# Token shift moved into the projection's eviction, and a new order of work inside a recurrent round

## The reference, cut to what matters

```python
h = rms_norm(x, g_pre)
z = h @ w_in
zs, zg_r, q, k, v, qi, ki, wi, zg_a, m_r, m_a = _split(z, SPLITS)
...
prev = jnp.concatenate([shift0[:, None, :].astype(zs.dtype), zs[:, :-1]], axis=1)
xs = zs + (prev - zs) * mu_shift
r, k, v, zw, za = _split(xs, (R_WIDTH, R_WIDTH, R_WIDTH, DECAY_RANK, ICLR_RANK))
w_log = -jax.nn.softplus(-(w0 + jnp.tanh(zw) @ w2).astype(f32)) - 0.5
a = jax.nn.sigmoid((a0 + za @ a2).astype(f32))
kk = k * ph(k_k); kk = kk / jnp.maximum(jnp.sqrt(jnp.sum(kk * kk, ...)), 1e-12)
k = k * (1.0 + (a - 1.0) * ph(k_a))
y, s_final = rwkv7_scan(r, decay, k, v, kk, kk * a, s0)
... group norm of y, plus sum(r * k * r_k) * v, times silu(zg)
return y, s_final, zs[:, -1]        # the last unshifted row is an output too
```

## Time and profile before

| what | value |
|---|---|
| time, median of 3 runs (lowest, highest) | 3446.24 us (3445.89, 3452.47) |
| profiled execution, its own time | 3446.67 us |
| its span, first to last instruction | 3445.1 us |
| busy: PE, DVE, ACT, POOL | 3162.6, 2162.1, 1105.0, 521.5 us |
| 0 to 1454 us (fro): PE, DVE, ACT, POOL busy | 1428.4, 1127.6, 331.9, 105.9 us |
| 1454 to 2087 us (attention): the same | 551.7, 405.6, 273.9, 112.5 us |
| 2087 to 2621 us (rwk): the same | 400.0, 362.5, 350.4, 243.6 us |
| 2621 to 3446 us (merge): the same | 782.5, 266.4, 148.8, 59.5 us |

### The profile page before, as it was taken

How to read it: one execution, slowest core, us unless ns; L and a number is a source line. 1 busy time by engine, 2 the same in 40 slices (tenths; PEclk the granted TensorE clock), 3 DMA queues, 4 the chain that set the end, 5 groups by cost and what they waited for, 6 DMA issues and landing times. The chain is left out here.

```text
span 3445.1 us, 66198 instructions
## 1 busy us (share of the span) xinstructions
PE 3162.6 (92%) x25784; PEld 1917.1 (56%) x25784; DVE 2162.1 (63%) x4342; ACT 1105.0 (32%) x2313; POOL 521.5 (15%) x732
## 2 busy tenths in 40 slices
PE   8999999999999999869999865877876999999998
PEld 4544445555555555446666544777765555555553
DVE  2017889999999999658776554677772444432221
ACT  4135660000000000135555324677762211111221
POOL 3331000000000000021111132455542000000000
PEclk9999999999999999979999976889897999999999
DMA  5232111111111111132111181222215211221110
GB/s 161 72 93 66 43 41 57 56 55 58 55 57 62 55 58 55 59 96 67 43 44 33 49 271 47 57 62 66 64 31 158 100 52 54 64 78 58 49 40 25
DMA packets 215817, 233.54 MB, mean 68 GB/s; under 512 B 28665, under 2 KB 191028, under 8 KB 215012
## 3 DMA queue, kind: packets, MB, share of 16 engines
q1 hardware_dynamic: 147960, 110.07, 11.8%
q0 software_dynamic: 23696, 59.79, 6.0%
q10 hardware_dynamic: 43868, 59.62, 5.0%
HBM read 158.75 MB, written 70.63 MB: 67 GB/s over the span
## 5 line engine op out<-in xcount | busy, mean ns | idle before, releaser
L409 PE MATMUL fro_acc<-h_t,fro_w 128*128 128x416 f32 x3280 | 1174.6, 516 | 0.0
L409 PEld LDWEIGHTS fro_acc<-h_t,fro_w 128*128 128x128 f32 x3280 | 614.5, 190 | 543.1 <-issue 536.1
L692 DVE TENSOR_SCALAR_CACHE_REDUCE fro_work<-scores,fro_real 128x384 uint8<-128x384 f32 (+6 forms) x462 | 656.2, 1474 | 2.1
L516 ACT ACTIVATE fro_out<-fro_acc 128x416 f32<-128x416 f32 (+3 forms) x230 | 118.0, 513 | 794.1 <-PE fro_acc L409 711.6
L3105 DVE CUSTOM_DVE_ANT_0 att_seen<-att_ps,scores 128x512 f32<-128x512 f32 (+3 forms) x320 | 181.4, 608 | 99.8 <-PE att_ps L2991 99.5
L2169 PE MATMUL mrg_po<-mrg_wo,mrg_mrg 128*128 128x512 f32 (+1 forms) x544 | 238.8, 597 | 4.6 <-DVE mrg_mrg L2274 4.6
L2201 PE MATMUL mrg_pg<-mrg_wg,mrg_x_t 128*128 128x512 f32 (+1 forms) x544 | 236.3, 592 | 0.0
L658 DVE SCALAR_TENSOR_TENSOR scores<-fro_work,w_idx,scores 128x512 f32<-128x512 f32 (+3 forms) x280 | 188.0, 671 | 39.2 <-ACT fro_work L573 12.2
L3075 ACT ACTIVATE att_seen<-att_seen,att_shift 128x128 f32<-128x128 f32 (+15 forms) x128 | 152.6, 1194 | 83.2 <-DVE att_shift L3113 83.2
L2169 PEld LDWEIGHTS mrg_po<-mrg_wo,mrg_mrg 128*128 128x128 f32 (+1 forms) x544 | 101.5, 187 | 139.1 <-issue 134.1
L573 ACT ACTIVATE fro_work<-fro_wk 128x512 f32<-128x512 f32 (+3 forms) x320 | 144.5, 540 | 90.7 <-PE fro_wk L482 89.8
(11 more groups left out here) (449 smaller groups left out, 4523.5 us busy)
## 6 DMA issues: line engine op xcount, KB each, us to landing
z_t<-fro_out ACTq DMA_DIRECT2D x180, 208.0 KB
fro_w<-in_w_in SPq DMA_DIRECT2D x41, 512.0 KB, 4.1
mrg_m_in<-z_t POOLq DMA_DIRECT2D x56, 256.0 KB, 3.5
scores<-in_cache_kv POOLq DMA_DIRECT2D x108, 128.0 KB, 3.1
rwk_zi<-z_t SPq DMA_DIRECT2D x80, 129.0 KB, 2.6
z_t<-fro_out ACTq DMA_DIRECT2D x45, 192.0 KB
scores<-in_x_prompt SPq DMA_DIRECT2D x16, 512.0 KB, 8.4
mrg_x<-in_x_prompt SPq DMA_DIRECT2D x16, 512.0 KB, 3.5
```

Of the source, the lines that this page charges most:

```text
L409: last = pe.matmul(acc[e % 2][:, 0:CW], w[block_no % 3][:, kk, :], h_t[:, kk, CW * g:CW * g + CW], start=(kk == 0), stop=(kk == KD - 1))
L692: chain.mark(dve.tensor_scalar(junk[b % 2][:, 0:n], scores[:, c:c + n], realf[:, b:b + 1], None, op, ALU.add, accum_out=count[:, b:b + 1]))
```

## The change: what it does, and the diff

The token shift is taken out of the recurrent stage and done once, in fro, when the 65 accumulators of the shifted blocks are evicted. For such an accumulator ACT now makes three copies where it made one: the raw columns into `out[:, 1:]`, the columns scaled by 1 - mu into `shifted`, and one column (zero, or the last of the group before) into `out[:, 0]`; the last group of a block adds a one-column copy into `tail`. POOL multiplies `out` by mu and adds it to `shifted`, and ACT starts the DMA of shifted group i-1 at the end of the eviction of group i, waiting for POOL (`mixed`). `out` of a shifted group is free when POOL has mixed it, no longer when a DMA has landed. POOL gets its own copy of the list of steps, with `store_keys` and `load_qi` dealt between the shifts.

In the recurrent stage `zi`, `pm`, `own_part`, `shifted` and `add_parts` are gone; SP loads `xs` and `vx` ready-made into three buffers each. ACT's `take_square(1)` and `take_keys` now stand ahead of `exps`, `take_square(2)` ahead of `spread_norms` and `take_values`; PE's `norms` come behind `square(3)`; DVE's `power(3)` comes ahead of `unit_key` and `mixed_key`, and `power(4)` behind them but ahead of `scaled_keys`. The zero column of `z_t` is no longer written, and the output of the last raw row comes from `tail`.

```diff
@@ fro, GpSimd
-            for q in range(NT - 1):
-                store_keys(q)
+            def shift(i):
+                e, j, g = E_SHIFT + i, i // CG, i % CG
+                m = CW if g < CG - 1 else CP
+                mu = PR["mu_shift"][0] + j
+                pool.wait_ge(raw_ok, i + 1)
+                pool.wait_ge(first_ok, i + 1)
+                pool.tensor_tensor(out[e % 3][:, 0:m], out[e % 3][:, 0:m], k.param[:, mu:mu + 1].to_broadcast([P, m]), ALU.mult).then_inc(faded, 1)
+                pool.wait_ge(faded, i + 1)
+                pool.wait_ge(evicted, e + 1)
+                pool.tensor_tensor(shifted[i % 2][:, 0:m], shifted[i % 2][:, 0:m], out[e % 3][:, 0:m], ALU.add).then_inc(mixed, 1)
...
             load_qi(0)
             load_qi(1)
-            store_keys(NT - 1)
+            shift_steps(2)
+            for gr in range(2):
+                for b in range(4):
+                    shift_steps(2)
+                for half in range(2):
+                    shift_steps(5)
+                if gr == 0:
+                    store_keys(0)
+            shift_steps(5)
+            for n in range(NT):
+                shift_steps(2)
+                if n >= 1:
+                    store_keys(n)
             store_keys(NT)
-            for b in range(2, NT):
-                load_qi(b)
+            for u, (b, sl, width) in enumerate(index_units()):
+                if sl == 0 and 2 <= b + 1 < NT:
+                    load_qi(b + 1)
+                for four in range(2):
+                    shift_steps(pace[2 * u + four])
+            shift_steps(B_STEPS)
@@ fro, ScalarE
+            def store_shift(i):
+                e, j, g = E_SHIFT + i, i // CG, i % CG
+                m = CW if g < CG - 1 else CP
+                act.wait_ge(mixed, i + 1)
+                act.dma_start(z_t[j, :, 1 + CW * g:1 + CW * g + m], shifted[i % 2][:, 0:m]).then_inc(shift_stored[i % 2], 16)
...
+                if is_shift(e):
+                    i = e - E_SHIFT
+                    act.activation(o[:, 1:1 + m], acc[e % 2][:, 0:m], ACT.Copy).then_inc(raw_ok, 1)
+                    if g == CG - 1:
+                        act.activation(tail[:, j:j + 1], acc[e % 2][:, m - 1:m], ACT.Copy).then_inc(tailed, 1)
+                    if i >= 2:
+                        act.wait_ge(shift_stored[i % 2], 16 * (i // 2))
+                    act.activation(shifted[i % 2][:, 0:m], acc[e % 2][:, 0:m], ACT.Copy, scale=keep_mu[:, j:j + 1]).then_inc(evicted, 1)
...
+                    act.activation(o[:, 0:1], first, ACT.Copy).then_inc(first_ok, 1)
+                    if i:
+                        store_shift(i - 1)
+                    return
@@ rwk, SyncE
-                sp.dma_start(zi[:, w, :], z_rows[:, w, m * P:m * P + P + 1]).then_inc(z_in[i], 16)
+                sp.dma_start(xs[m % 3][:, w, :], z_rows[:, w, m * P + 1:m * P + 1 + P]).then_inc(x_in[m % 3], 16)
...
@@ rwk, ScalarE, a round
-                if inputs:
-                    own_part(n + 3, 0)
...
+                if inverse:
+                    take_square(n + 1, 1)
                 if features:
                     exps(n + 2)
+                if inverse:
+                    take_keys(n + 1)
+                    take_square(n + 1, 2)
+                if features:
                     spread_norms(n + 2)
                     take_values(n + 2)
-                if inverse:
-                    take_square(n + 1, 1)
-                    take_keys(n + 1)
-                if features:
                     key_mix(n + 2)
-                if inverse:
-                    take_square(n + 1, 2)
...
@@ rwk, VectorE, a round
-                if inputs:
-                    add_parts(n + 3, 0)
...
+                if inverse:
+                    power(n + 1, 3)
                 if features:
                     unit_key(n + 2)
                     mixed_key(n + 2)
                 if inverse:
-                    power(n + 1, 3)
-                if inputs:
-                    add_parts(n + 3, 1)
+                    power(n + 1, 4)
                 if features:
                     scaled_keys(n + 2)
-                if inverse:
-                    power(n + 1, 4)
-                if features:
                     scaled_rows(n + 2)
```

192 lines of the change are left out of this document (99 added, 93 removed).

## The result

The changed kernel takes 3473.99 us, the median of 6 runs (3465.26 to 3481.24); the kernel before took 3450.31 beside it (6 runs, 3445.89 to 3455.53). The ratio is 1.0074, 95% interval 1.0057 to 1.0091: slower. The forecast was 3457, the range 3428 to 3480. The profiled execution of the changed kernel took 3472.84 us, its span is 3471.2, so the two profiled executions differ by 26.2 us.

| | before, us | after, us | change | forecast |
|---|---|---|---|---|
| first stage ends (DVE copies `sst_cur`) | 1454.6 | 1480.6 | +26.0 | +45.5 |
| recurrent stage set up (DVE's first line) | 2087.9 | 2116.1 | +28.2 | +45.5 |
| merge starts (PE's first branch) | 2633.2 | 2661.1 | +27.9 | +10 |
| recurrent stage, set-up to merge | 545.3 | 545.0 | -0.3 | -35.5 |
| span | 3445.1 | 3471.2 | +26.1 | +10 |

A forecast was written before the change was run, and what follows sets the result against it. PE's list was taken to bound the first stage and merge, the chain of waits in a round the recurrent stage. First stage +45.5 and recurrent -35.5 gave +10 on 3446.67, so 3457 us, range 3428 to 3480.

The forecast's parts named there:

- stay above 28.7: Recurrent rounds: the forecast counts as wrong if they fall below 27 or stay above 28.7 us.
- Part 1: First stage: ACT's longer eviction, 65 times a copy of 0.5 us and a column of 0.2, costs nothing.
- Part 2: First stage, pages: ACT waits for POOL behind its page loads, delaying page copies; +7.5 us, bounds 4 to 11.5.
- Part 3: First stage, key tiles: stores behind shifts delay DVE's copies; 2.9 us three times, last 3.3; +11, bounds 3 to 16.
- Part 4: Index stretch: POOL's shifts lock out DVE's multiply-adds, 1.5 us each, 28 times, less 15 of slack; +27, bounds -1 to 53.
- The end of the stage moves by the same 27: First stage: DVE's 27 us of delay in the index stretch reach PE and move the stage's end equally.
- The search: Threshold search: passes read one input, so nothing counted; the rival that they are held up, +15 us, had 0.07.
- Part 6: Start of the recurrent stage: ready inputs start PE 4.5 us sooner, the second round gains 1; -5.5 us.
- Part 5: Recurrent rounds: new order and removed work gain 14 x 2.1 + 0.6 = 30 us; bounds 0.8 to 3.5 a round.
- So 27.65 a round: Recurrent stage: forecast length of a round in us, against 29.8 before.
- The rival of the late keys: Recurrent rounds: chain keys, product, sums, side gives 1 us a round instead of 2.1; stage -20, sum 3472; chance 0.12.

The follow-up runs named there:

- POOL small: Changed kernel with POOL's two operations of each shift on 8 columns instead of 384 or 416, the other columns' mix left out; 3449.99 us.
- order alone: Kernel before with only the new order of the rounds, shift still in the recurrent stage, DVE's input additions ahead of the keys; 3525.77 us.
- keys first: Changed kernel with each key tile's two stores issued ahead of the shift of the same iteration, not behind it; 3456.08 us.
- the mean of five (259.5): Profiles of five kernels in which the changed kernel's first stage stands unchanged; index stretch 256.6 to 263.3 us.
- the lightly filled one: Changed kernel with 2, 4, 4 and 7 unread matmuls ahead of squares 0, 1, 3 and the bonus sums of each round; 3444.18 us.
- five profiles: Profiles of five kernels in which the changed kernel's rounds stand unchanged; set-up to merge 527.0 to 545.0 us, mean 535.6.
- the old order: Changed kernel with ACT's, DVE's and PE's order of before put back into the rounds; 3458.93 us.
- the filled kernel's: Changed kernel with the order of before in the rounds and 3, 4 and 8 unread matmuls ahead of squares 0, 1 and 2; 3457.29 us.

## Where the prediction was right and where it was wrong, step by step

It forecast a slower kernel, 3457 us in a range of 3428 to 3480, and 3473.99 was measured. That the time lies in the range is luck: the first stage lost 19.5 us less than forecast and the recurrent stage gained 35.2 us less, and the two misses have opposite signs. By the prediction's own sign, rounds that "stay above 28.7", its rounds were wrong on average: their mean is 29.9, though seven of the 15 lie below 28.7.

- **Part 1, ACT's eviction, 0:** borne out. POOL small has the longer eviction and takes 249.8 us in the index stretch, order alone has the eviction of before and takes 250.1, both with 6.8 us at the low clock.
- **Part 2, the pages, +7.5:** right, +7.8, by the mechanism named; the wait for page 8's DMA went as well.
- **Part 3, the key tiles, +11:** the mechanism was right (keys first shows it), the size +8.4. The pauses are 2.18, 2.25 and 2.11, not 2.9, and the last 2.37, not 3.3; one of 1.15 that was not forecast stands between them (276.93), and 1.6 us of DMA waits of before are gone.
- **Part 4, the lock, +27:** the mechanism was right, the term mis-sized: +9.7 in the profile, +12.6 by the mean of five (259.5). Some 3 of the 9.7 are the low clock, which the part did not count. DVE lost 1.03 us a shift (28.8 / 28) instead of 1.5, and got 8.9 back from its waits instead of 15: from its first multiply-add to its last it took 16.7 us more (266.2 against 249.5), not 27. Then the sentence "The end of the stage moves by the same 27" fails: DVE's last multiply-add stands 10.9 us behind PE's last dots (549.0 and 538.1), before 3.9 (516.1 and 512.2), and those 7 us and more are swallowed by DVE's wait at the end of the stage, 17.22 instead of 27.53. The prediction named that wait as a cover for small things, and then did not set DVE's delay against it. The Trainium skill's rule (SBUF — State Buffer, SBUF: two separate sides) calls the shared pair an exclusive lock for whole instructions. The trace agrees in kind: POOL's addition takes 1.40 beside DVE and 1.06 without. But a shift's 1.9 us on POOL are not all lost to DVE, since POOL does part of the waiting: in the index stretch its two instructions take 1.02 and 1.35 on average, in the search 0.87 and 1.05, which makes 0.45 a shift. DVE lost 54% of the 1.9.
- **The search, 0:** right, 656.2 us in both, and POOL did not wait there either: 0.87 and 1.05, as short as beside an idle DVE (0.89 and 1.06 at 207.99).
- **Part 6, the start, -5.5:** -4.7 (the first transpose of the ladder 40.8 behind the set-up, before 45.5).
- **Part 5, the rounds, -30:** this is the step that failed. "So 27.65 a round" agrees with the rounds at the full clock: 27.6 in the changed kernel's undisturbed rounds and a mean of 27.7 in the lightly filled one, whose stage gained 33.4 where 35.5 were forecast. But the working took each duration of PE from one round of before and let the clock be what it was there. In the changed kernel 7 of 15 rounds are at 1.2 GHz for 10 to 17 us behind the pause at the bonus sums, at 3 to 6 us each: first to last ladder took 3.6 us more, not 30 less, in the profiled execution, and 3.8 less by the mean round of five profiles (29.4). The rival of the late keys had the right place (recurrent stage -20, against -0.3 here and -9.7 in the mean of five), but its mechanism, a chain that gains only 1, did not occur: `side` came 2.3 sooner. What the late keys do is make the pause. How much of the 2.1 us a round the new order was worth is not shown: order alone came out spoiled, and with the inputs ready the old order took 26.9 us in its three rounds at the full clock, and 27.0 to 29.0 in the filled kernel's.

The Trainium skill (TensorE: Matmul & The Clock Gate, Part 1: The HAM clock gate) has the clock follow how busy TensorE has recently been, and names two levels for it, 1.2 and 2.4 GHz, as long as no more than two cores of a die are busy. The rows agree: 0.50 and 1.00 in the stretches of the round of 32.7 us. The prediction did not weigh the clock at all in its rounds.

The stretches between the marks add up, as they must: 7.8 + 8.4 + 9.7 + 2.2 (the attention stage) - 0.3 - 1.8 (the merge, 811.9 before and 810.1 after) = 26.0 of the 26.1 by which the spans differ.
